# An encoder layer's feed-forward part as two-by-two block products: seven products where there were eight, tokens in two groups

## The reference

```python
h = rmsnorm(x, norm1_g)
proj = h @ w_in                      # q (8 heads), k, v (2 heads), pool input u
a = block_swept_gqa(rope(rmsnorm(q)), rope(rmsnorm(k)), v)
p = multiscale_pool(u, w_pool, pool_scale)
x = x + concatenate([a, p]) @ w_out
h2 = rmsnorm(x, norm2_g)
x = x + square(relu(h2 @ w_up)) @ w_down     # w_up 1024 x 4096, w_down 4096 x 1024
```

## Time and profile before

| | us |
|---|---|
| median of 3 runs | 1652.85 (1651.77 to 1652.86) |
| profiled execution, first to last instruction | 1650.2 |
| what lies between that span and the median | 2.65 |
| last output projection matmuls begin (chain of waits) | 595.99 |
| last addition into `yacc` begins (chain of waits) | 1645.95 |

### The profile page before, as it was taken

How to read it: one execution, slowest core, us unless ns; L and a number is a source line. 1 busy time by engine, 2 the same in 40 slices (tenths; PEclk the granted TensorE clock), 3 DMA queues, 4 the chain that set the end, 5 groups by cost and what they waited for, 6 DMA issues and landing times.

```text
span 1650.2 us, 20830 instructions
## 1 busy us (share of the span) xinstructions
PE 1616.3 (98%) x7904; PEld 1352.0 (82%) x7904; DVE 826.7 (50%) x933; ACT 508.3 (31%) x808; POOL 304.2 (18%) x305
## 2 busy tenths in 40 slices
PE   7999989999999999999999999999999999999998
PEld 6999868888778888888888888888888888888887
DVE  6434489999764344434443443444434434433443
ACT  5223289999832231112112111211121112111210
POOL 3324667888810000000000000000000000000000
PEclk9999999999999999999999999999999999999999
DMA  5100021000132251100100100001001000010003
GB/s 219 57 29 18 15 86 27 13 10 13 61 119 90 75 214 80 51 26 25 51 25 25 51 25 25 25 25 51 25 25 51 25 25 27 26 49 25 25 0 153
DMA packets 24033, 82.14 MB, mean 50 GB/s; under 512 B 2496, under 2 KB 4672, under 8 KB 21952
## 3 DMA queue, kind: packets, MB, share of 16 engines
q1 hardware_dynamic: 24000, 81.70, 14.2%
HBM read 64.39 MB, written 12.58 MB: 47 GB/s over the span
## 4 chain that ended last, share of the span: by engine, by line
PE 87%; POOL 4%; DVE 3%; ACT 2%; issue 2%; DMA 1%; SPq 0%; POOLq 0%; ACTq 0%; DVEq 0%
PE ps L537 24%; PE ps L539 24%; PE ps L538 24%; PE ps L733 4%; PE ps L635 3%; PE ps L739 2%; POOL prob L1488 1%; PE ps L650 1%; PE ps L651 1%; PE ps L617 1%; PE ps L619 1%; DVE nmax L1159 1%; PE ps L748 1%; DVE wolo L1104 1%; PE ps L546 1%
## 5 line engine op out<-in xcount | busy, mean ns | idle before, releaser
L1365 DVE TENSOR_TENSOR yacc<-yacc,ps 128x1024 f32<-128x1024 f32 x192 | 234.3, 1220 | 229.3 <-PE ps L539 229.3
L1075 ACT ACTIVATE relu<-ps 128x512 f32<-128x512 f32 x96 | 57.5, 599 | 840.0 <-PE ps L539 840.0
L537 PE MATMUL ps<-h2hi,wuhi 128*128 128x512 f32 x768 | 298.9, 389 | 0.0
L539 PE MATMUL ps<-h2hi,wulo 128*128 128x512 f32 x768 | 298.8, 389 | 0.0
L538 PE MATMUL ps<-h2lo,wuhi 128*128 128x512 f32 x768 | 298.8, 389 | 0.0
L537 PE MATMUL ps<-wdhi,hid_hi 128*128 128x512 f32 x768 | 298.8, 389 | 0.0
L538 PE MATMUL ps<-wdlo,hid_hi 128*128 128x512 f32 x768 | 298.8, 389 | 0.0
L539 PE MATMUL ps<-wdhi,hid_lo 128*128 128x512 f32 x768 | 298.8, 389 | 0.0
L1354 DVE TENSOR_TENSOR hsq<-relu 128x512 f32<-128x512 f32 x96 | 66.4, 692 | 351.9 <-ACT relu L1075 351.9
L537 PEld LDWEIGHTS ps<-wdhi,hid_hi 128*128 128x128 f32 x768 | 144.1, 188 | 30.0
L539 PEld LDWEIGHTS ps<-h2hi,wulo 128*128 128x128 f32 x768 | 144.1, 188 | 30.0
(11 more groups left out here) (117 smaller groups left out, 2198.2 us busy)
## 6 DMA issues: line engine op xcount, KB each, us to landing
wuraw<-in_w_up SPq DMA_DIRECT2D x16, 1024.0 KB, 4.8
wdraw<-in_w_down SPq DMA_DIRECT2D x16, 1024.0 KB, 4.9
xin<-in_x SPq DMA_DIRECT2D x12, 512.0 KB, 3.4
x2in<-in_x SPq DMA_DIRECT2D x12, 512.0 KB, 3.6
out_y<-x2in SPq DMA_DIRECT2D x12, 512.0 KB, 2.9
yacc<-out_y SPq DMA_DIRECT2D x3, 2048.0 KB, 13.0
woraw<-in_w_out SPq DMA_DIRECT2D x2, 2048.0 KB, 8.0
out_y<-yacc SPq DMA_DIRECT2D x2, 2048.0 KB, 6.6
```

The lines of the kernel that those rows point to most:

```text
L537: pe.matmul(out, w_hi, m_hi, start=start, stop=False)
L539: return pe.matmul(out, w_lo, m_hi, start=False, stop=stop)
L1365: dve.tensor_tensor(yacc[:, t], yacc[:, t], psw[:, r:r + 1024], ALU.add).then_inc(acc_done, 1)
```

## The change

The hidden columns of a chunk (256), the width (1024) and the output columns (1024) are each seen as two halves, and a product of two-by-two blocks is made from seven block products in place of eight. The operands of the seven are blocks or sums of blocks, so sums are formed before the split: of the weights on POOL (`sum_wu`, `sum_wd`, four sums of 128x512 each a chunk), of the hidden values on DVE (`sum_hid`), and of the normalized input once, behind the second norm, on DVE. For the up product the results of the seven are combined in PSUM and by three additions (`save_u` copies on ACT, `sum_u` on DVE); the seven down products are ordered so that they add up in PSUM and are taken out after each one (`accumulate`, 128x1536).

Fourteen operand blocks (hi and lo of seven) of the input for 1536 tokens do not fit in SBUF. So tokens go in two groups of 768 (`TOK` = 384 per block), the second half of the tiles first, and the weights are fetched, summed and split once for each group: `CHUNKS` = 32 steps. The operands of the other group are kept in DRAM (`h2d`) and fetched between the groups, and `yacc` is stored and fetched there too.

A step on PE now alternates an up product of chunk n+1 (12 matmuls of 384 columns) with a down product of chunk n (9 matmuls of 512 columns), seven times. The lo parts of `w_up` are made by POOL (`lo_wu`), no longer by DVE. Each of the seven operands has one buffer.

The core of the diff (semaphores, the second norm's new sums, the exchange between the groups and the last steps are left out):

```diff
+TOK = QT_TILES * P
+CHUNKS = 2 * NCH
+ORDER = (0, 3, 1, 4, 2, 5, 6, 9, 7, 10, 8, 11)
...
+        SLOTS = 7
+        OPENS = (0, 1, 3)
+        QUARTERS = ((0, 0), (0, 0), (1, 0), (1, 1), (1, 1), (1, 0), (0, 1))
+        HID_ORDER = (0, 1, 2, 3, 4, 6, 5)
...
+            def load_wu(n, c):
+                sp.wait_ge(wu_lo, FIRST + SLOTS * n)
+                sp.dma_start(wuraw[:], w_up[bass.ds(c, 1)].rearrange("a p k f -> (a p) k f")).then_inc(wu_in, 16)
+            def load_wd(n, c):
+                sp.wait_ge(wd_lo, FIRST + SLOTS * n)
+                sp.dma_start(wdraw[:], w_down[bass.ds(c * FC, FC)].rearrange("(f p) (h n) -> p f h n", p=P, h=2)
+                             ).then_inc(wd_in, 16)
...
+            with sp.Fori(0, NCH - 2) as n:
+                load_wd(n + 1, n + 1)
+                load_wu(n + 2, n + 2)
...
...
+            def up_product(n, o):
+                pe.wait_ge(wu_lo, FIRST + SLOTS * n + o + 1)
...
+                if o == 0 and not (isinstance(n, int) and n == 0):
+                    pe.wait_ge(relu_done, 4 * n)
+                if o == 1 and not (isinstance(n, int) and n == 0):
+                    pe.wait_ge(u_sum, 3 * n)
+                if o == 2:
+                    pe.wait_ge(u_copied, 3 * n + 1)
+                if o == 3:
+                    pe.wait_ge(u_sum, 3 * n + 1)
+                if o == 4:
+                    pe.wait_ge(u_copied, 3 * n + 2)
+                if o == 5:
+                    pe.wait_ge(u_copied, 3 * n + 3)
+                if o == 6:
+                    pe.wait_ge(u_sum, 3 * n + 2)
+                out = ps[:, 6 + o % 2, 0:TOK].rearrange("p (q c) -> p q c", q=QT_TILES)
+                for k in range(4):
+                    mm = three(out, wuhi[o][:, k], wulo[o][:, k], h2[o][:, 0, :, k], h2[o][:, 1, :, k],
+                               o in OPENS and k == 0, k == 3, o not in OPENS)
+                mm.then_inc(up_done, 1)
+            def down_product(n, o):
+                pe.wait_ge(wd_lo, FIRST + SLOTS * n + o + 1)
+                pe.wait_ge(hid_lo, SLOTS * n + in_order(HID_ORDER, o))
+                if o == 0:
+                    pe.wait_ge(acc_done, FIRST + SLOTS * n)
+                elif o > 1:
+                    pe.wait_ge(acc_done, FIRST + SLOTS * n + o - 1)
+                for q in range(QT_TILES):
+                    tok = slice(q * P, (q + 1) * P)
+                    mm = three(ps[:, QT_TILES * (o % 2) + q], hidhi[o][:, tok], hidlo[o][:, tok], wdhi[o][:], wdlo[o][:],
+                               o in OPENS, True, o not in OPENS)
+                mm.then_inc(down_done, 1)
+            def mlp_step(n):
+                for o in range(SLOTS):
+                    up_product(n + 1, o)
+                    down_product(n, o)
+            up_product(0, 0)
+            up_product(0, 1)
+            transpose_x2(TT - 1)
+            for o in range(2, SLOTS):
+                up_product(0, o)
+            with pe.Fori(0, NCH - 1) as n:
+                mlp_step(n)
+            mlp_step(NCH - 1)
+            with pe.Fori(NCH, CHUNKS - 1) as n:
+                mlp_step(n)
+            for o in range(SLOTS):
+                down_product(CHUNKS - 1, o)
...
+            def hi_wu(n, o):
+                if not (isinstance(n, int) and n == 0):
+                    act.wait_ge(up_done, FIRST + SLOTS * (n - 1) + o + 1)
+                if o in (0, 1, 5):
+                    act.wait_ge(wu_in, 16 * n + 16)
+                else:
+                    act.wait_ge(wu_sum, 4 * n + {2: 3, 3: 2, 4: 1, 6: 4}[o])
...
+            def square_relu(n, k, out):
+                if k < 3:
+                    act.wait_ge(u_sum, 3 * n + k + 1)
+                    src = usum[:]
+                else:
+                    act.wait_ge(up_done, FIRST + SLOTS * n + SLOTS)
+                    src = ps[:, 6, 0:TOK]
...
+                act.activation(relu[:], src, ACT.Relu).then_inc(relu_done, 1)
+                act.wait_ge(relu_done, 4 * n + k + 1)
+                if not (isinstance(n, int) and n == 0):
+                    act.wait_ge(hid_lo, SLOTS * (n - 1) + {0: 5, 1: 7, 2: 6, 3: 5}[k])
+                act.activation(out[:], relu[:], ACT.Square).then_inc(raw_done, 1)
+            def save_u(n, k):
+                act.wait_ge(up_done, FIRST + SLOTS * n + (1, 3, 4)[k])
...
+                copy((ucopy, u2, ucopy)[k][:], ps[:, (6, 6, 7)[k], 0:TOK]).then_inc(u_copied, 1)
+            def mlp_step(n, up=True, wu=True, wd=True):
+                u = n + 1
+                if up:
+                    save_u(u, 0)
+                if wu:
+                    hi_wu(n + 2, 0)
+                if wd:
+                    hi_wd(n + 1, 0)
+                if up:
+                    square_relu(u, 0, h11)
+                if wu:
+                    hi_wu(n + 2, 1)
+                if wd:
+                    hi_wd(n + 1, 1)
+                if up:
+                    hi_hid(u, 0)
+                    save_u(u, 1)
+                if wu:
+                    hi_wu(n + 2, 2)
+                if wd:
+                    hi_wd(n + 1, 2)
+                if up:
+                    save_u(u, 2)
+                if wu:
+                    hi_wu(n + 2, 3)
+                if wd:
+                    hi_wd(n + 1, 3)
+                if up:
+                    square_relu(u, 1, h22)
+                if wu:
+                    hi_wu(n + 2, 4)
+                if wd:
+                    hi_wd(n + 1, 4)
+                if up:
+                    square_relu(u, 2, h21)
+                    hi_hid(u, 1)
+                if wu:
+                    hi_wu(n + 2, 5)
+                if wd:
+                    hi_wd(n + 1, 5)
+                if up:
+                    square_relu(u, 3, h12)
...
+            def sum_u(n, k):
+                dve.wait_ge(up_done, FIRST + SLOTS * n + (2, 5, 6)[k])
...
+                dve.wait_ge(u_copied, 3 * n + (1, 3, 2)[k])
+                a, e = ((ucopy, 7), (ucopy, 6), (u2, 7))[k]
+                dve.tensor_tensor(usum[:], a[:], ps[:, e, 0:TOK], ALU.add).then_inc(u_sum, 1)
+            def sum_hid(n, k):
+                dve.wait_ge(raw_done, 4 * n + 4)
...
+                if k >= 2:
+                    dve.wait_ge(hid_sum, 4 * n + (1, 3)[k - 2])
+                out, a, b, op = ((hid_s[4], h12, h22, ALU.add), (hid_s[3], h11, h12, ALU.subtract),
+                                 (hid_s[2], hid_s[4], h11, ALU.subtract), (hid_s[6], h21, hid_s[2], ALU.subtract))[k]
+                dve.tensor_tensor(out[:], a[:], b[:], op).then_inc(hid_sum, 1)
+            def lo_hid(n, o):
+                dve.wait_ge(hid_hi, SLOTS * n + in_order(HID_ORDER, o))
+                src = {0: h11, 1: h21, 5: h22}[o] if o in (0, 1, 5) else hid_s[o]
+                minus(hidlo[o][:], src[:], hidhi[o][:]).then_inc(hid_lo, 1)
+            def lo_wd(n, o):
+                dve.wait_ge(wd_hi, SLOTS * n + o + 1)
+                if o in (2, 4):
+                    dve.wait_ge(wd_sum, 4 * n + 4)
+                src = {0: wdraw[:, 0, 0], 1: wdraw[:, 1, 0], 2: wd_t2[:], 3: wdraw[:, 0, 1],
+                       4: wd_t1[:], 5: wdraw[:, 1, 0], 6: wdraw[:, 1, 1]}[o]
+                minus(wdlo[o][:], src, wdhi[o][:]).then_inc(wd_lo, 1)
+            def accumulate(n, o, g):
+                half, h = QUARTERS[o]
+                dve.wait_ge(y_in[2 * half + h], 16 * g + 16)
+                dve.wait_ge(down_done, FIRST + SLOTS * n + o + 1)
+                if o in (1, 4):
+                    dve.wait_ge(acc_done, FIRST + SLOTS * n + o)
+                b = QT_TILES * (o % 2)
+                dve.tensor_tensor(acc_quarter(half, h), acc_quarter(half, h), ps[:, b:b + QT_TILES], ALU.add
+                                  ).then_inc(acc_done, 1)
+            def mlp_step(n, g, down=True, up=True):
+                u = n + 1
+                if down:
+                    accumulate(n, 0, g)
+                    lo_hid(n, 3)
+                    lo_hid(n, 4)
+                if up:
+                    sum_u(u, 0)
+                if down:
+                    accumulate(n, 1, g)
+                    lo_hid(n, 6)
+                    lo_hid(n, 5)
+                if up:
+                    lo_wd(u, 0)
+                    lo_wd(u, 1)
+                if down:
+                    accumulate(n, 2, g)
+                if up:
+                    lo_hid(u, 0)
+                    lo_wd(u, 2)
+                if down:
+                    accumulate(n, 3, g)
+                if up:
+                    sum_u(u, 1)
+                    lo_wd(u, 3)
+                if down:
+                    accumulate(n, 4, g)
+                if up:
+                    sum_u(u, 2)
+                    lo_wd(u, 4)
+                if down:
+                    accumulate(n, 5, g)
+                if up:
+                    lo_hid(u, 1)
+                    lo_wd(u, 5)
+                    for k in range(3):
+                        sum_hid(u, k)
+                if down:
```

(67 more changed lines are left out.)

587 lines of the change are left out of this document (337 added, 250 removed).

## The result

The changed kernel takes 1880.8 us (median of 4 runs, 1879.7 to 1881.4) against 1652.3 us of the kernel before on the same chip: 1.139 times as long, 95% interval 1.137 to 1.140. The forecast was 1865 us. PE has 121 us less of matmuls at full clock, and the kernel is 228 us longer, since the engines that feed PE now set the step.

What follows compares the result with a forecast made beforehand. The prediction took a loop through SP's transfers, POOL, DVE and ACT as the bound, 38.4 us a step: 614.7 + 1228.8 - 10.8 + 11 + 19 = 1862.7, plus 2.65, 1865 us; range 1730 to 1945 us.

Steps and rivals of the forecast that it cites:

- a loop over SP, POOL, DVE and ACT: Feed-forward step, from one wdlo6 to the next through transfers and engine queues: 35.0 us without collisions, 38.4 with them.
- 636.5 + 32 x step: Whole kernel: the time in us as a fixed part plus 32 feed-forward steps, 1865 us in all.
- the exchange: Between the two token groups: stored and fetched operands and sums delay wuraw and wdraw, about +11 us.
- -10.8: Last step: no wuraw (2.8 us) and four POOL operations in place of ten (8.0 us).
- POOL, ten operations, with meetings: Loop part from wuraw's landing: ten operations of 1.34 us, 13.4, plus three collisions with DVE of 0.55, 1.7.
- DVE, wdlo2 to the second usum, wdlo2 meeting POOL: Loop part after POOL's tenth operation: two lo parts, two additions, two usums, 5.4 us, plus one collision, 1.3.
- DVE, hidden sums to wdlo6, meetings, semaphores: Loop's last part: sums, addition 6 and wdlo6 4.2 us, collisions counted 0.4 of 1.3, semaphores 0.3.
- PE's stops: PE in each step: idle about 5 us ahead of up product 5 and about 4 ahead of down product 0.
- rival 2: Slower clock: matmuls after PE's stops run at half rate, 41 to 43 us a step, 1950 to 2010 us; chance 0.15.
- Rival 1: The loop without collisions: 33.9 to 35.0 us a step, 1721 to 1757 us; chance 0.22, including down to 1708.
- Rival 3: PE stays the bound, only down product 0 waits: 29.4 us a step, 1577 us, faster than before; chance 0.07.
- What would show it: Signs in the changed profile: PE idle 9 to 10 us a step, wuraw about 8 us behind wdlo6, POOL operations 1.3 to 1.5.

Runs made afterwards that it cites:

- e2: Changed kernel with DVE's 18 two-input operations a step made one-input ones of the same length (wrong results): 1741.9 us.
- e6: Changed kernel, four order changes: w_up fetched before w_down; last addition, then wdlo6, before hidden sums; POOL's w_down sums earlier: 1664.6 us.
- e10: e9 plus wdlo2 moved behind addition 3 and the second usum on DVE: 1604.7 us, 0.972 of the kernel before.
- e3: Changed kernel without the hi by lo matmul, the second of three, in every feed-forward product: 1861.2 us.
- e5: Changed kernel with DVE's last addition of a step moved ahead of the three hidden sums: 1875.3 us.
- e8: e6 plus e2's edit, one-input operations on DVE (wrong results): 1594.1 us, 0.965 of the kernel before.
- e1: Changed kernel with SP issuing the w_up transfer ahead of the w_down transfer: 1786.6 us.
- e9: e6 plus the four hidden lo parts moved ahead of the first addition on DVE: 1613.7 us.

## Why the prediction was right, and where its sizes were off

The mechanism held: the step is a loop over SP, POOL, DVE and ACT, not a sum on one engine. The formula 636.5 + 32 x step gives 1881.3 us with the measured step of 38.9 ((1080.33 - 691.29) / 10), against 1880.8, so start, exchange and end were right as a sum. That is partly luck. The start was right: SP's first issue of wdraw in the loop is at 653.32 us, where 614.7 + 38.4 + 0.2 = 653.3 was forecast. The two steps around the exchange were 9.2 us longer than the others and not 11. From SP's last issue of wdraw (1828.66) to the end of the span it is 50.7 us and not 46. In the faster kernels the formula is too low, by 11 us for e2, 17 for e6 and 24 for e10: the last step does not shrink with the others, as the forecast's -10.8 had it (50.7 us behind SP's last issue of wdraw in the changed kernel, 51.4 in e6, 52.4 in e10), and in e10 the three steps around the exchange are 17 us longer than the others.

The terms of one step, between ends and starts in the timelines of DVE, POOL and ACT (wdlo6 ends 885.71):

| part | forecast | measured |
|---|---|---|
| SP, wdraw, wuraw behind it | 7.9 | 7.5 (to 893.22) |
| POOL, ten operations, with meetings | 13.4 + 1.7 | 14.8 (to 907.99) |
| DVE, wdlo2 to the second usum, wdlo2 meeting POOL | 5.4 + 1.3 | 6.7 (to 914.65) |
| ACT, relu to square | 3.8 | 3.7 (to 918.36) |
| DVE, hidden sums to wdlo6, meetings, semaphores | 4.2 + 0.4 + 0.3 | 6.2 (to 924.53) |
| sum | 38.4 | 38.8 |

The first four are within 0.4 us each. The fourth was not what ended last, though: ACT's square ended at 918.36, and DVE, whose own queue held wdlo4, addition 5, hidlo1 and wdlo5, began the hidden sums at 919.22. The last row is the mis-sized term: "Of wdlo4, hidlo1 and the hidden sums one may meet POOL's last two: 1.3, of which I count 0.4". All three met one of POOL's last three. DVE's timeline:

```profile
917.15 1.55 DVE L1336 TENSOR_TENSOR hidlo<-h,hidhi 128x384 fp32r<-128x384 f32 x1
...
919.22 2.10 DVE L1619 TENSOR_TENSOR hid_s<-h,h 128x384 f32<-128x384 f32 x2
```

and POOL's beside it:

```profile
916.98 1.30 POOL L1904 TENSOR_TENSOR wulo<-wuraw,wuhi 128x512 fp32r<-128x512 f32 x1 [1.97 <-ACT wuhi L941]
918.96 1.48 POOL L1904 TENSOR_TENSOR wulo<-wuraw,wuhi 128x512 fp32r<-128x512 f32 x1 [0.68 <-ACT wuhi L941]
```

POOL's last three lo parts don't follow its tenth operation in a row, as I had placed them: each waits for ACT's hi part, so they are spread over the very stretch in which DVE makes wdlo4, hidlo1 and the sums. wdlo4 lost 0.3 us, hidlo1 1.0 and the two sums 1.1; without the first two, DVE would have ended wdlo5 at about 918.0 us, ahead of ACT's square. All meetings together were 4.7 us (e2), where 3.4 was taken and 0 to 5 allowed.

**PE's stops.** Forecast about 5 us ahead of up product 5 and 4 ahead of down product 0. Measured: 2.4 us a step for the first (31.7 us in 13 steps), 3.4 for the second, and about 1 for down products in between. The first is the part that was mis-sized, and the clock is some of the reason. The forecast put slow matmuls behind rival 2 only; they came, but in PE's slack. PE's timeline behind the 3.4 us stop of one step:

```profile
884.78 0.76 PE L653 MATMUL ps<-wdhi,hidhi 128*128 128x512 f32 x1 [3.39 <-DVE yacc L1642]
885.35 0.63 PE L654 MATMUL ps<-wdlo,hidhi 128*128 128x512 f32 x1
885.77 0.63 PE L655 MATMUL ps<-wdhi,hidlo 128*128 128x512 f32 x1
...
890.36 0.52 PE L655 MATMUL ps<-h,wulo 128*128 128x384 f32 x1
890.68 0.46 PE L653 MATMUL ps<-h,wuhi 128*128 128x384 f32 x1
890.98 0.34 PE L654 MATMUL ps<-h,wuhi 128*128 128x384 f32 x1
891.15 0.34 PE L655 MATMUL ps<-h,wulo 128*128 128x384 f32 x1
```

The distance is 0.43 us for 512 columns and 0.32 for 384 up to 890.7, the level of 1.2 GHz, then 0.17 for 384. Nine wide and six narrow matmuls at 0.20 and 0.15 us above their full-clock distance are 2.7 us that PE would otherwise have idled later in the step, and its stop ahead of up product 5 is 1.0 us. Not every step is like this one. In two of the ten steps from 691 to 1080 us PE has no slow matmul behind nearly the same stop (3.3 us, ending at 807.17 and at 1001.65), and its next stop, ahead of up product 5, is 3.6 us (at 829.81 and 1024.26):

```profile
807.17 0.47 PE L653 MATMUL ps<-wdhi,hidhi 128*128 128x512 f32 x1 [3.30 <-DVE yacc L1642]
807.48 0.40 PE L654 MATMUL ps<-wdlo,hidhi 128*128 128x512 f32 x1
```

Six steps lie between, with a stop of 2.5 us; in the one of 729.08 us, for example, the slow matmuls take 1.7 us more than at full clock. So the clock explains why the mean is 2.4 us and not 3.6; why it is 3.6 and not 5 where no matmul is slow stays open. Rival 2's 41 to 43 us a step were wrong: e3, which takes a third of PE's matmuls and lowers its clock to 0.81, and e5, which moves its longest stop, change the kernel's time by 20 and 6 us.

**Rival 1** (no collisions, 33.9 to 35.0 us a step, 1721 to 1757 us) was wrong about the kernel and right about its own number: e2, which has none, took 34.2 and 1742 us. **Rival 3** (PE stays the bound at 29.4 us) needed another order and no meetings: e8 has 29.4 us a step, with 1594 us and not 1577. That the two numbers agree is luck. The rival had PE wait for the last addition, 4.25 us against a slot of 4.1, which would make 29.0 or 29.1 us and not 29.4; e8's PE does not wait at all, and its products alone take 29.4 us. e10 comes within 0.2 us of it with its two-input operations left in. That their meetings now fall where DVE has slack is my reading of its busy times (330 us of 350 on DVE, 349.5 on PE), not tested alone.

**What would show it.** POOL's first operation waits for wuraw (yes), wuraw lands about 8 us behind wdlo6 (7.5), DVE's largest wait is wdlo2's for POOL (67.5 us, yes), lo parts above 0.69 and 0.56 us and sums with them (1118 and 1509 ns, yes). POOL at 1.3 to 1.5 us was right on the mean of all (1.42) but not group by group (1.27 to 1.67), and PE's idle time missed (6.8 us and not 9 to 10).

**Small slips in the working.** 11 operations at 0.46 us and 7 at 0.59 are 9.2 us, not 9.4, so the two engines' two-input work is 28.1 us; nothing else rests on it. And the row of 0.69 us at 220.49 was not without company: POOL began an operation 0.06 us behind it (220.55). What the row shows is that DVE's operation kept its length where it began first.

**Left open.** The loop's second path through ACT's wuhi1 was seen in e1's timelines and was shortened in e6 by its move on POOL, together with the other edits; it was not moved alone. The moves in e6 were not weighed one by one beyond e1 and e5: together they gave 216 us (1880.8 to 1664.6), far more than the 94 and 6 us of these two alone, which is what one expects where several paths are nearly equally long.

## What to carry to other kernels

An edit that takes work off the busiest engine has to be costed as a loop: follow one buffer from the operation that frees it to the next that frees it, through every queue it passes, and compare that length with the busy time of the engine that is to stay the bound. Each operation stands in a queue behind waits that are not its own, and several loops are often almost as long: one reordering alone gave 6 to 94 us here, the six of e10 together 276. Two-input operations on DVE and POOL that touch SBUF are to be counted where both run (they cost 4.7 us of a step of 38.9 here), and it may be worth placing them where the engine has slack, which e9 and e10 suggest and no run tests alone.

## What the runs showed of the hardware that was not expected

- Meetings were as long as the one in the rows of before (1.67 us against 0.69), but hit far more operations: a lo part of 384 columns took 1509 ns on the mean of 39 against 545 for an operation of the same size with one input, and two neighbours of 512 took 3.47 us and not 1.3. A reduction over an axis of length one reads one input, takes the same time as the two-input operation alone (683 and 545 ns) and neither slows POOL (1295 ns) nor is slowed by it.
- With a stop of 3.4 us once a step of 39 us PE ran the 5.9 us behind it (884.8 to 890.7) at the level of 1.2 GHz, and the mean granted clock is 0.94; the stops of 1.0 and 1.6 us in the same step have matmuls at full speed behind them. Nearly the same stop (3.3 us) ahead of 807.17 and of 1001.65 has full speed behind it (clock 1.00 from 807.1 to 811.0 and from 1001.6 to 1006.0), and a shorter one (2.9 us, ahead of 690.18) has 16 slow matmuls behind it, so the length of one stop does not tell by itself what the clock will do. In e3_two, with a third of the matmuls gone, the mean fell to 0.81.
- PE's distance between matmuls of 384 columns is 0.17 us (890.98 to 891.15), as the prediction interpolated between 256 and 512 (0.1735).
